# Time mix's scan: token-side matrices of direction 1 in the opposite partition half, both directions' products issued head by head

## The reference, cut to what matters

```python
def _wkv7_step(S, inp):
    r, w, k, v, kk, a = inp
    sa = jnp.einsum('bhvk,bhk->bhv', S, kk)
    S = S * w[:, :, None, :] - sa[..., None] * (kk * a)[:, :, None, :] + v[..., None] * k[:, :, None, :]
    y = jnp.einsum('bhvk,bhk->bhv', S, r)
    return S, y
...
    _, y_fwd = lax.scan(_wkv7_step, S0, (r_t, tm(decay[0]), tm(kd[0]), v_t, kk_t, tm(a[0])))
    _, y_bwd = lax.scan(_wkv7_step, S0, (r_t, tm(decay[1]), tm(kd[1]), v_t, kk_t, tm(a[1])), reverse=True)
    y = jnp.swapaxes(y_fwd + y_bwd, 0, 1)
```

## Time and profile before

| what | us |
|---|---|
| median of 3 executions | 2681.8 (2680.28 to 2685.88) |
| the profiled execution, its own time | 2691.59 |
| its span in the trace | 2689.7 |
| mean granted TensorE clock | 0.972 of full speed |
| PE busy | 2553.0 (95%) |
| DVE busy, ACT busy | 1985.5 (74%), 1525.1 (57%) |

### The profile page before, as it was taken

How to read it: one execution, slowest core, us unless ns; L and a number is a source line. 1 busy time by engine, 2 the same in 40 slices (tenths; PEclk the granted TensorE clock), 3 DMA queues, 4 the chain that set the end, 5 groups by cost and what they waited for, 6 DMA issues and landing times. The chain is left out here.

```text
span 2689.7 us, 47740 instructions
## 1 busy us (share of the span) xinstructions
PE 2553.0 (95%) x20277; PEld 2105.1 (78%) x20277; DVE 1985.5 (74%) x2847; ACT 1525.1 (57%) x2207; POOL 175.6 (7%) x192
## 2 busy tenths in 40 slices
PE   8999999989997999999999999998999899999988
PEld 7779997689965666767676766766969899978888
DVE  7855549655346999999998989896747875756874
ACT  5535424323124777878787877775446554446453
POOL 0000000020001440000000000100200201200201
PEclk9989999999988999999999999999999999999999
DMA  7315543310032999999999999993625544625542
GB/s 198 102 63 174 176 136 116 115 43 4 4 139 83 374 373 373 372 375 371 373 367 379 378 371 375 351 402 111 204 63 166 178 128 140 202 63 165 172 139 95
DMA packets 264614, 565.87 MB, mean 210 GB/s; under 512 B 25996, under 2 KB 204356, under 8 KB 221260
## 3 DMA queue, kind: packets, MB, share of 16 engines
q1 hardware_dynamic: 257580, 547.02, 58.0%
q0 software_dynamic: 5248, 10.23, 1.2%
q10 hardware_dynamic: 1568, 5.51, 0.6%
HBM read 545.41 MB, written 11.53 MB: 207 GB/s over the span
## 5 line engine op out<-in xcount | busy, mean ns | idle before, releaser
L319 DVE TENSOR_TENSOR wl<-raw,wh 128x1024 fp32r<-128x1024 f32 (+1 forms) x610 | 741.8, 1223 | 302.3 <-ACT wh L310 286.9
L310 ACT ACTIVATE wh<-raw 128x1024 fp32r<-128x1024 f32 (+1 forms) x610 | 640.4, 1054 | 471.6 <-PE PS L163 415.2
L319 DVE TENSOR_TENSOR wl<-early,wh 128x1024 fp32r<-128x1024 f32 x384 | 466.7, 1230 | 52.7 <-ACT wh L310 34.5
L310 ACT ACTIVATE wh<-early 128x1024 fp32r<-128x1024 f32 x384 | 405.4, 1060 | 125.3 <-PE PS L163 104.8
L161 PE MATMUL PS<-wh,xe_h 128*96 128x512 f32 x896 | 356.9, 398 | 6.8 <-DVE wl L319 5.0
L161 PE MATMUL PS<-b_hn_h,wh 128*128 128x256 f32 (+1 forms) x1152 | 339.4, 295 | 21.2 <-DVE wl L319 14.5
L163 PE MATMUL PS<-wh,xe_l 128*96 128x512 f32 x896 | 353.7, 395 | 0.0
L162 PE MATMUL PS<-wl,xe_h 128*96 128x512 f32 x896 | 353.6, 395 | 0.0
L162 PE MATMUL PS<-b_hn_l,wh 128*128 128x256 f32 (+1 forms) x1152 | 332.5, 289 | 0.0
L163 PE MATMUL PS<-b_hn_h,wl 128*128 128x256 f32 (+1 forms) x1152 | 332.4, 289 | 0.0
L161 PEld LDWEIGHTS PS<-b_hn_h,wh 128*128 128x128 f32 (+1 forms) x1152 | 225.8, 196 | 27.6 <-DVE wl L319 16.8
(11 more groups left out here) (494 smaller groups left out, 4942.1 us busy)
## 6 DMA issues: line engine op xcount, KB each, us to landing
early<-in_moe_in SPq DMA_DIRECT2D x128, 1024.0 KB, 6.9
raw<-in_moe_in SPq DMA_DIRECT2D x96, 1024.0 KB, 7.2
raw<-in_w_in SPq DMA_DIRECT2D x76, 1024.0 KB, 5.5
early<-in_moe_out SPq DMA_DIRECT2D x64, 1024.0 KB, 7.2
raw<-in_moe_out SPq DMA_DIRECT2D x48, 1024.0 KB, 6.6
raw<-in_attn_w_in SPq DMA_DIRECT2D x24, 512.0 KB, 5.4
raw<-in_rw_w_rkv SPq DMA_DIRECT2D x12, 1024.0 KB, 5.1
raw<-in_ffn_w_gate SPq DMA_DIRECT2D x11, 1024.0 KB, 5.3
```

The costliest lines, as they stand in the source:

```text
L310: act.e.activation(st.two(n)[0], st.raw(n), ACT.Copy).then_inc(*act.sig("hi", st.name, n, sem=f"hi_{st.name}"))
L319: dve.e.tensor_tensor(lo, st.raw(n), hi.bitcast(F32), SUB).then_inc(*dve.sig("lo", st.name, n, sem=f"lo_{st.name}"))
```

## The change

It does two things. Token-side matrices of direction 1 move to the other half of the partitions: `token(d, x)` is the half of head parity `x` in direction `d`, 64·(x XOR d). A product that goes from features to tokens, or from tokens to features, so goes straight (half 0 to 0, 1 to 1) in direction 0 and across (0 to 1, 1 to 0) in direction 1. And `first`, `pre`, `res`, `out` and `grow` take a step `s` instead of a group: both groups' banks are taken first, and the products are issued for a pair of heads of direction 0, then the same pair of direction 1, and so on. Products that go from tokens to tokens (`AKP`·`VT` in `res`, `upd`, `level`) and from features to features (`sm`·`RE` in `out`) stay straight in both directions. In `res` and `out` these come first, for the whole of both groups, and PE then waits for its own semaphore (`res.begun`, `y.begun`) before it adds the other products to the same sums. `VT` is now made for each group, ten times, since each direction needs it in its own half. `pre(s)` waits for both directions' `ka` and `re` before its first product.

```diff
-    for c, (u, o) in {0: (3, 1344), 4: (5, 1344), 1: (0, 0), 3: (0, 512), 2: (0, 1024)}.items():
-        VT[c] = heads3(f"sc_vt{c}", 64, u_at(u) + 4 * o)
+        VT.append(heads3(f"sc_vt{n}", 64, u_at(u) + 4 * 1344))
...
+        def token(d, x):
+            return 64 * (x ^ d)
...
+        def pre(s):
+            for d in range(2):
+                pe.wait_ge(pe.at("prep", d, "ka"))
+                pe.wait_ge(pe.at("prep", d, "re"))
             for nm, a_, b_ in (("akp", KA, KE), ("arp", KA, RE), ("abq", BE, RE)):
...
+                bs = [take(nm, g) for g in PAIRS[s]]
+                for f in range(KC):
+                    for (g, d, ci), b in zip(both_of(s), bs):
+                        t = slice(ci * CH, ci * CH + CB_)
+                        for x in range(2):
+                            p, q_ = 64 * x, token(d, x)
+                            m = e.matmul(PS[q_:q_ + CB_, b, f * CB_:(f + 1) * CB_], a_[d][p:p + 64, f, t],
+                                         b_[d][p:p + 64, f, t], start=True, stop=True)
...
-                if g + 2 >= len(groups) if nm != "vt" else VT_BY[ci] != g:
+            for nm, src in (("kt", KA), ("bt", BE), ("vt", (rw_v, rw_v))):
+                if nm != "vt" and s == NCH - 1:
                     continue
...
-            for h in range(16):
-                p, f = half(h)
-                o = PS[p:p + CB_, b, f * 64:(f + 1) * 64]
-                e.matmul(o, AKP[g % 2][p:p + CH, f, :], VT[ci][p:p + CH, f, :], start=True, stop=False)
-                x = e.matmul(o, KE[d][p:p + 64, f, t], sm[d][p:p + 64, f, :], start=False, stop=True)
-            x.then_inc(*pe.sig("scan_mm", "res", g))
+            bs = [take("res", g) for g in PAIRS[s]]
+            for (g, d, ci), b in list(zip(both_of(s), bs))[::-1]:
+                for f in range(KC):
+                    for x in range(2):
+                        q_ = token(d, x)
+                        m = e.matmul(PS[q_:q_ + CB_, b, f * 64:(f + 1) * 64], AKP[d][q_:q_ + CH, f, :],
+                                     VT[d][q_:q_ + CH, f, :], start=f == 0, stop=False, skip_group_check=True)
+                m.then_inc(*pe.sig("scan_mm", "res.begun", g))
+            pe.wait_ge(pe.at("scan_mm", "res.begun", 2 * s + 1))
+            for f in range(KC):
+                for (g, d, ci), b in zip(both_of(s), bs):
+                    t = slice(ci * CH, ci * CH + CB_)
+                    for x in range(2):
+                        p, q_ = 64 * x, token(d, x)
+                        m = e.matmul(PS[q_:q_ + CB_, b, f * 64:(f + 1) * 64], KE[d][p:p + 64, f, t], sm[d][p:p + 64, f, :],
+                                     start=False, stop=True, skip_group_check=True)
...
+        def out(s):
+            for g in PAIRS[s]:
+                pe.wait_ge(pe.at("upd", g))
+                pe.wait_ge(pe.at("abq", g))
...
+        def pre(s):
+            for nm, dst, sc_ in (("kt", KT, 1.0), ("bt", BT, -1.0), ("vt", VT, 1.0)):
+                if nm != "vt" and s == NCH - 1:
+                    continue
+                for g in PAIRS[s]:
+                    act.wait_ge(act.at("scan_mm", nm, g))
```

More of the change, by code:

```diff
@@ L950, in levels @@
                         level(g, l, part)
[L951 to L954, removed]
+        for s in (2, 3):
+            first(s)
+        pre(0)
         back(0)
@@ L957, in scan_order @@
         for s in range(NCH):
-            both_ = (2 * s, 2 * s + 1)
-            for g in both_:
-                res(g)
+            res(s)
             if s == 0:
@@ L965, in scan_order @@
             if s == 1:
-                for g in WAVES[2]:
-                    first(g)
-            for g in both_:
+                first(4)
+            for g in PAIRS[s]:
                 upd(g)
@@ L973, in scan_order @@
                 forward(2)
-            for g in both_:
-                out(g)
+            out(s)
             if s < 2:
@@ L978, in scan_order @@
             if s + 1 < NCH:
-                for g in both_:
-                    grow(g)
+                grow(s)
             if s < 2:
@@ L983, in scan_order @@
             if s + 1 < NCH:
-                for g in both_:
-                    pre(g + 2)
+                pre(s + 1)
             if s == 1:
@@ L1183, in upd @@
             x.then_inc(*pe.sig("scan_mm", "upd", g))
[L1185 to L1197, removed]
@@ L1212, in rwkv_pe @@
             if u == 3:
-                for g in WAVES[0]:
-                    first(g)
+                for s in range(2):
+                    first(s)
             if u == 5:
@@ L1548, in level @@
                 e.tensor_tensor(x, x, ps56(nm, g, 0), SUB).then_inc(*dve.sig(nm, g, 0))
-        def pre(g):
-            d, ci = groups[g]
-            for nm, dst, mk in (("akp", AKP, f"strict{d}"), ("arp", ARP, f"incl{d}"), ("abq", ABQ, f"neg{d}")):
-                dve.wait_ge(dve.at("scan_mm", nm, g))
-                if g == 1:
-                    dve.wait_ge(dve.at("bonus.kd"))
-                if g >= 2:
-                    dve.wait_ge(dve.at("scan_mm", "y", g - 2))
-                e.tensor_tensor(dst[g % 2], ps56(nm, g), mask(mk), MUL).then_inc(*dve.sig(nm, g))
@@ new lines, in out, with grow @@
+        def out(s):
+            for g in PAIRS[s]:
+                d, ci = groups[g]
+                yv, src = rw_y[:, :, ci * CH:ci * CH + CH], ps64("y", g)[:, :, 0:CH]
+                dve.wait_ge(dve.at("scan_mm", "y", g))
+                if g < 5:
+                    e.tensor_copy(yv, src).then_inc(*dve.sig("y", g))
+                else:
+                    dve.wait_ge(dve.at("y", 9 - g))
+                    e.tensor_tensor(yv, yv, src, ADD).then_inc(*dve.sig("y", g))
+        def grow(s):
+            for g in PAIRS[s]:
+                d, ci = groups[g]
+                dve.wait_ge(dve.at("scan_mm", "grown", g))
+                e.tensor_tensor(sm[d], sm[d], ps64("grown", g), ADD).then_inc(*dve.sig("grown", g))
+                dve.wait_ge(dve.last)
+                e.tensor_tensor(sm[d], sm[d], bc(fac[d][:, :, ci if d == 0 else ci - 1], [128, KC, 64], 2), MUL).then_inc(
+                    *dve.sig("state", g + 2))
```

188 lines of the change are left out of this document (103 added, 85 removed).

## The result

Side by side on one chip the changed kernel takes 2701.4 us (median of 11 runs, 2689.8 to 2704.9) and the kernel before 2685.3 us (11 runs, 2679.9 to 2688.7). The ratio is 1.0057, interval 1.0045 to 1.0069, so it is slower by 0.57%, some 15 us; the forecast was 16 us faster. The profiled execution is one of the quickest of its runs: 2694.49 us.

A forecast was written before the change was run, and what follows sets the result against it. PE was taken to bound the scan nearly everywhere; the terms from the start through step 4 summed to -18.4 us, with 2.4 for the clock -16, giving 2665.8 us for the runs, range 2658 to 2690.

The forecast's parts named there:

- the price: Time per small record on PE when four quarters run: taken as half of today's 25.9 to 29.3 ns.
- slower rival: Four quarters don't overlap further, PE starts small records no faster than today, only costs remain: +17, 2699 us; chance 0.20.
- the clock: New pauses of PE ahead of `pre(0)` and in steps 0 and 1 bring 1.2 GHz spells: 0 to 5 us, 2.4 taken.
- Start to the first `res`: `first` and `pre(0)` up to `back(0)`: cheaper records, less the wait for both `RE`: -5.5 us.
- The wait for both `RE`: Ahead of `pre(0)`, PE waits for DVE's multiplications for both directions: +1.2 us.
- Step 0: `res` and `out` get shorter, but DVE's and ACT's chain sets the end, so `grow` and `pre(1)` bring nothing: +0.4 us.
- Step 1: `first` and `out` gain, PE then waits for banks DVE frees, `level` starts some 3 us earlier: -3.7 us.
- Step 2: No solving; `out` -0.7, `grow` -1.9, `res` -0.35, and the last bank for `level` free 4.7 us earlier: -5.0 us.
- Step 3: `out` -1.1, `grow` -1.9, then `pre(4)` with two more `vt`; `res` waits for the ninth `vt` copy: -3.8 us.
- Step 4: `out` -1.1, and +0.35 for the first bank behind it: -0.8 us.
- the walk: Step-by-step sum along the scan's path, using row durations and having PE wait for every bank in turn: -18.4 us.
- 0.55, 0.04 and two thirds of 0.16: Chances of the forecast (2659 to 2673), a larger gain (2660), and four quarters only partly faster (2672 to 2683), summed as faster.

The follow-up runs named there:

- run 1: Six streams of 256 small products each (one half, two halves, four quarters; 8, 56 or 112 columns) added ahead of the kernel before's scan; four quarters at 56: 29 to 31 ns a record.
- run 2: The changed kernel with direction 1's token-side matrices back in the same half, so only two products run side by side: 2707.8 us, ratio 1.0090.
- run 7: The changed kernel with `AKP` and `ARP` made by one product of 112 columns, 320 records fewer: 2697.0 us, ratio 1.0031.

## Why the prediction was wrong

**The step that failed** is the price. It was said to lie "between half of today's (12.9 to 14.6 ns) and the whole of it", and half was taken because `spread` scales by 2.0. Half is right for 128 records and wrong for a stream. `spread` has 32 records, 64 instructions in 3.88 us, and could not show a limit of 256 in 3.4 us or more. In streams four-fold records took 27 to 31 ns (run 1; `pre(1)` of the changed kernel). The text had the right numbers in hand, in its slower rival: one packet of 16 KB for 256 instructions, and products that would ask for them twice as fast. What it didn't do is compare: 128 records at 25.9 ns are 3.3 us, and 4 to 6 GB/s in every stretch of the scan is one packet per 3 to 4 us. The chance of 0.20 for that rival was too small for a limit that stood in each row.

The rival's own time, 2699 at a median before of 2681.8 (+17), is close to the measured +16, but partly by luck. It assumed no gain from four quarters at all; run 2 shows +24 without them and 9 given back by them. And 8 of the 16 go with the clock, which the forecast had at +2.4 and the rival not at all; why the clock is lower stays open.

**The sum, term by term** (forecast; difference of the two profiles). Start to the first `res`: -5.5; -0.3 (529.9 to 589.1 before, 530.5 to 589.4 after). PE after, in order of time, `pre(0)` and the start of `back`, and its waits for "issue" in `level` (L1121), 553 to 589 us:

```profile
555.23 4.21 PE L1151 MATMUL PS<-rw,rw 64*56 64x56 f32 x192 [4.58 <-DVE rw L1533]
559.15 1.36 PE L1164 MATMUL PS<-CB,rw 64*56 64x64 f32 x64
...
563.15 0.94 PE L1164 MATMUL PS<-CB,rw 64*56 64x64 f32 x50 [0.83 <-issue]
564.02 1.20 PE L1103 MATMUL PS<-CB,sc_pad 128*128 128x128 f32 x9
```

```profile
PE PS L1121 <- issue: 0.9, 3, 0.5
```

The wait for both `RE` came (4.58 us, and a start 0.25 us later than in the earlier trace rows). But the first 192 records take 3.9 us and not 2.5, since a spell at 1.2 GHz falls on them (PEclk is 0.51 from 555.9 to 559.4 us). `back` begins 1.4 us earlier than in the earlier trace rows, and by the first `res` that is gone too. Step 0: +0.4; -1.0. Step 1: -3.7; +1.3, with the spell of 10.2 us. Step 2: -5.0; +2.3. Step 3: -3.8; +1.8. Step 4: -0.8; -0.4. Sum: -18.4 (without the clock); +3.7. So the walk was within 1.4 us where other work is the bound (step 0, by masks and copies) or where streams are short (step 4), and wrong by 5 to 7 us wherever the term was "n records at half price" in `grow` and `pre`. The forecast's own sums have small slips that decide nothing: the terms told for step 0 add up to +0.9, not +0.4, and 0.55, 0.04 and two thirds of 0.16 to 0.70, not 0.68.

**What was right.** Four quarters do run together. PE's busy time fell by 40 us against 45. The second copies cost 0.9 us ahead of `out`, as forecast. The wait on PE's own semaphore, 0.3 us in the forecast, costs nothing visible in the rows at 624.69, where the first records of the second part start before the last of the first part. Two pauses of 0.5 us ahead of the second part of `out` (L1221, steps 3 and 4) have no releaser in the profile and may be this wait or a block's. "Of 45 us less work, 27 turn into waiting" had the right form and the wrong number: all 40 did.

**The rule of the slower rival.** The Trainium skill ("TensorE: Matmul & The Clock Gate", Wait — 56ns, not 53.3ns?) has a floor of about 25 ns from one start to the next, however few the columns. As a floor of the array the runs refute it: 128 starts come 13 ns apart at 56 columns, and 8 ns at 8 columns and 1.2 GHz. As a mean over a long stream the number is near: 27 to 31 ns here. Who had gone by it would have forecast 2692 and the right sign.

## What to carry to other kernels

Ahead of any change that makes small products faster, divide the instructions of a stretch by 256 and the time by that: in this scan, stretches at 3.4 to 4 us a block were bound by the instructions, whatever PE's busy share said. Fewer and larger instructions shortened it (run 7); faster ones in long streams did not. A price seen in a burst is not the price of a stream; look for the longest row of the kind, and for how often its packets come. Short streams behind a wait still gained (3.7 us against 5.6 for one `out`), so weigh each stretch by its length, and count what the new order makes both sides wait for (up to 18 us here) first.

## What the hardware showed that was not expected

- PE's instructions came in packets of 16 KB, 256 instructions each, and four-fold streams ran in bursts of 128 records, 3.45 us apart at the least and 3.7 to 4.0 us in most (run 1 and the changed kernel). Between the bursts PE stood for 1.9 to 2.3 us, and the profile calls it "issue". Two-fold streams of 26 ns a record (512 of them in run 1) showed no pause.
- Four quarters of the array reach 13 ns a record at 56 columns, a quarter of the 51.7 ns of one half, in bursts. With 8 columns, at 1.2 GHz, one half takes 27 ns and four quarters 8.
- Records of different quarters start out of the order in which they are issued (L1188 at 624.69 ahead of L1179 at 624.75).
- The time of a run goes with its mean clock, here 1.5 to 1.7 us for each 0.001; closely in the 11 runs of the changed kernel, loosely in the 13 of the kernel before.
